# Mixing of the first block redrawn: heads in pairs, a new column order, and a new order of work on three engines

## The reference, cut to what matters

```python
for l in range(2):                                   # first block
    proj = rms_norm(x, ln1) @ w_in                   # 1024 -> 23 column chunks of 128
    mq, mk = rope(rms_norm(mq)), rope(rms_norm(mk))  # per head of 64
    y_moba = causal softmax attention, 6 heads       # one block of 256 keys
    qk = silu(causal_conv4(xqk));  i, f gates
    num = (q k^T * w) v;  den = sum(q k^T * w)       # w = exp(d - m_t), mLSTM, 4 heads
    h = num / max(|den|, exp(-m_t))
    y_mlstm = rms_norm(h * sigmoid(xo)) per head
    y_swa = windowed softmax attention with sinks, 6 query heads, 2 key heads
    x = x + concat(y_moba, y_mlstm, y_swa) @ w_out   # 8 row slabs of w_out
    x = x + relu(rms_norm(x) @ w_up)^2 @ w_down
```

## Time and profile before

| | us |
|---|---|
| three timed runs | 1591.03, 1581.5, 1591.17 (median 1591.03) |
| the profiled execution, its own time | 1587.58 |
| its span, from the first to the last instruction | 1585.7 |

### The profile page before, as it was taken

The page is one execution under the profiler, slowest core; times in us unless marked ns, Lnnn a source line. Parts: engine busy times, 40 slices in busy tenths (PEclk is TensorE's granted clock), DMA queues, the critical chain, the costliest instruction groups (busy, mean ns, idle before and its releaser), DMA issues.

```text
span 1585.7 us, 25621 instructions
## 1 busy us (share of the span) xinstructions
PE 1492.0 (94%) x10380; PEld 1366.3 (86%) x10380; DVE 1175.4 (74%) x1911; ACT 830.5 (52%) x1256; POOL 10.5 (1%) x21
## 2 busy tenths in 40 slices
PE   6987899999887999999999999999999999999997
PEld 5875788888875678888999899999899999999996
DVE  6677788886767778887756787788776678777753
ACT  4453577634444567644536555444554666455542
POOL 2000000000000000000000000000000000000000
PEclk9997999999898999999999999999999999999999
DMA  8441279996432159997745557789975555578662
GB/s 216 124 134 49 83 221 265 271 295 181 120 107 80 54 175 259 261 306 233 227 134 155 151 160 213 222 242 256 261 218 171 147 147 161 171 228 228 193 181 76
DMA packets 480422, 292.29 MB, mean 184 GB/s; under 512 B 13725, under 2 KB 452257, under 8 KB 480049
## 3 DMA queue, kind: packets, MB, share of 16 engines
q1 hardware_dynamic: 478928, 287.02, 63.0%
q10 hardware_dynamic: 672, 1.97, 0.3%
q0 software_dynamic: 704, 1.66, 0.3%
HBM read 289.56 MB, written 1.05 MB: 183 GB/s over the span
## 4 chain that ended last, share of the span: by engine, by line
PE 68%; DVE 20%; ACT 7%; issue 4%; DMA 0%; ACTq 0%; DVEq 0%
PE acc L1453 10%; PE mx L1470 10%; PE acc L1454 10%; PE acc L1455 10%; PE acc L1470 7%; DVE w_lo L815 6%; PE mx L1471 5%; PE acc L1471 4%; ACT w_hi L498 3%; DVE ada_acc L902 2%; PE mx L1501 1%; PE mx L1722 1%; PE mx L1711 1%; ACT gt L785 1%; DVE upv L1396 1%
## 5 line engine op out<-in xcount | busy, mean ns | idle before, releaser
L815 DVE TENSOR_TENSOR w_lo<-raw,w_hi 128x1024 fp32r<-128x1024 f32 x450 | 547.4, 1220 | 168.3 <-ACT w_hi L498 167.0
L1453 PE MATMUL acc<-h,w_hi 128*128 128x258 f32 (+1 forms) x1776 | 521.6, 294 | 11.8 <-DVE w_lo L815 9.7
L1454 PE MATMUL acc<-h,w_hi 128*128 128x258 f32 (+1 forms) x1776 | 508.4, 286 | 0.0
L1455 PE MATMUL acc<-h,w_lo 128*128 128x258 f32 (+1 forms) x1776 | 502.8, 283 | 0.0
L498 ACT ACTIVATE w_hi<-raw 128x1024 fp32r<-128x1024 f32 x450 | 460.3, 1047 | 37.2 <-DMA raw<-in_w_down 15.9
L1453 PEld LDWEIGHTS acc<-h,w_hi 128*128 128x128 f32 x1776 | 340.4, 192 | 23.6 <-DVE w_lo L815 10.1
L1454 PEld LDWEIGHTS acc<-h,w_hi 128*128 128x128 f32 x1776 | 341.2, 192 | 6.7 <-issue 6.3
L1455 PEld LDWEIGHTS acc<-h,w_lo 128*128 128x128 f32 x1776 | 343.4, 193 | 0.0
L1470 PE MATMUL mx<-u,w_hi 128*128 128x512 f32 x864 | 302.3, 394 | 2.1 <-DVE u L1402 2.1
L1471 PE MATMUL mx<-u,w_lo 128*128 128x256 f32 x864 | 241.5, 280 | 0.0
L1470 PEld LDWEIGHTS mx<-u,w_hi 128*128 128x128 f32 x864 | 162.2, 188 | 37.5 <-DVE u L1402 2.5
(11 more groups left out here) (272 smaller groups left out, 1731.8 us busy)
## 6 DMA issues: line engine op xcount, KB each, us to landing
raw<-in_w_in SPq DMA_DIRECT2D x132, 512.0 KB, 3.9
ada<-in_w_ada SPq DMA_DIRECT2D x96, 512.0 KB, 5.0
raw<-in_w_ffn_in SPq DMA_DIRECT2D x88, 512.0 KB, 4.6
raw<-in_w_up SPq DMA_DIRECT2D x64, 512.0 KB, 4.6
raw<-in_w_down SPq DMA_DIRECT2D x64, 512.0 KB, 5.3
raw<-in_w_out SPq DMA_DIRECT2D x32, 512.0 KB, 3.8
raw<-in_w_ffn_out SPq DMA_DIRECT2D x32, 512.0 KB, 4.5
raw<-in_w_ret_o SPq DMA_DIRECT2D x16, 512.0 KB, 4.0
```

The lines of the kernel that those rows point to most:

```text
L815: V.tensor_tensor(w_lo[:, n % NS], raw[:, n % NS], w_hi[:, n % NS].bitcast(F32), ALU.subtract).then_inc(lo_ready, 1)
L1453: mm(outp, w_hi[:, i % NS, k], rhs[:, k, 0], start=k == 0, stop=False)
L1454: mm(outp, w_hi[:, i % NS, k], rhs[:, k, 1], start=False, stop=False)
L1455: ins = mm(outp, w_lo[:, i % NS, k], rhs[:, k, 0], start=False, stop=k == KT - 1)
```

## The change

It is made in the mixing of the first block, in both layers.

- **Columns.** `A_ORDER` brings the chunks of the attention pairs earlier and mixed with the values. In `proj` the two chunks of a head-norm group now lie side by side (`A_PLACE`), and the swa keys are paired with another chunk. Projections use three `acc` banks; the fourth, `acc[:, 3]`, takes the sums, the partners and two of the values, one after the other.
- **Pairs.** Attention goes by six pairs of heads in the order 0, 1, 2, 4, 3, 5. Both heads of a pair have their matmuls interleaved (rows 0 to 63 and 64 to 127 of the array, or columns 0 to 63 and 64 to 127), one exponential phase, one set of maxima, six transposes into two banks, one copy. ml_scores and ml_outputs go by two heads as well.
- **Masks on PSUM.** A matmul of the rounded identity with the masks opens each bank of scores, and the scores are added to it. Maxima are read from PSUM (one reduction over 2 x 3 x 128), and the exponential reads PSUM too. The masks are loaded and rounded once, on ACT in layer 0.
- **Memory without division.** The root-mean-square norm of num / max(|den|, e) is taken without the quotient: m_d = max(den^2, e^2), v = sum(h^2) + 64 eps m_d, h * v^-1/2. The reciprocal and two passes go; `g_E` is exp(-2 G), clamped on DVE (`f_E2`). The first tap of the convolution moves to ACT (`conv_first`), the rounding of y_hi 3 and 4 as well.
- **Order.** The head norms, the memory and pairs 0 and 1 stand between the projections; pair 2 between `out_chunks`, of which slabs 0 to 3 first go with six of eight chunks. Slabs 6 and 7 go bank by bank at the end.
- **Constants.** The decay table shares its place with the masks' neighbours in `con` and is loaded in the MLP of layer 1, by the queue of GpSimd.

```diff
-A_ORDER = (22, 14, 15, 16, 17, 20, 21, 18, 19, *range(14))
+A_ORDER = (22, 14, 15, 16, 17, 20, 21, 0, 3, 18, 19, 1, 4, 6, 7, 2, 5, 8, 13, 10, 12, 9, 11)
+PAIRS = (0, 1, 2, 4, 3, 5)
+W_ORDER = (3, 4, 0, 1, 2, 6, 5, 7)
```

On ACT:

```diff
+                def conv_first(k):
+                    act.wait_ge(ap_ev, e0 + 2 + k)
+                    nc.scalar.activation(cv[:, k], proj[:, A_PLACE[C_XQK + k]], ACT.Identity, scale=vec(V_CONVW + l * 16 + 12 + k),
+                                         bias=vec(V_CONVB + l * 4 + k)).then_inc(cv_first, 1)
...
+                ahead(21)
+                head_square(2)
+                exps(0)
+                head_seed(2)
+                ahead(22)
+                turned(0)
```

On DVE:

```diff
+                def maxima(j):
...
+                    c.link(V.tensor_reduce(st_mx[:, i], mx[:, 0:2, 0:384].rearrange("p n (b k) -> p n b k", b=3), AX, ALU.max))
+                    c.link(V.tensor_tensor(st_mx[:, i, :, 1:2], st_mx[:, i, :, 1:2], st_mx[:, i, :, 2:3], ALU.max))
...
-                c.link(V.scalar_tensor_tensor(r_tmp[:], mx[:, 3], -1.0, ebc, ALU.mult, ALU.max))
-                c.link(V.tensor_tensor(r_tmp[:], mx[:, 3], r_tmp[:], ALU.max))
...
-                c.link(V.reciprocal(r_tmp[:], r_tmp[:]))
...
+                c.link(V.tensor_tensor(m_d, m_d, ebc[:], ALU.max))
+                to_sbuf(14)
+                head_norm(1)
+                dve.wait_ge(ml_ss, l + 1)
+                V.scalar_tensor_tensor(m_v, m_d, HD * EPS, mx[:, 0], ALU.mult, ALU.add).then_inc(ml_v, 1)
...
+                to_sbuf(16)
+                maxima(0)
+                rope(1)
...
+                to_sbuf(17)
+                probabilities(0)
+                head_norm(2)
+                to_sbuf(18)
+                maxima(1)
+                to_sbuf(19)
+                outputs(0)
+                rope(2)
+                probabilities(1)
...
+                maxima(3)
                 rope(4)
...
+                lo_upto(p0 + 29)
+                probabilities(3)
+                maxima(4)
+                lo_upto(p0 + 30)
+                outputs(3)
+                probabilities(4)
+                maxima(5)
+                outputs(4)
+                lo_upto(m0 + 1)
+                probabilities(5)
+                outputs(5)
```

On PE:

```diff
+                    for i in range(2):
+                        mm(mx[:, i, 0:384], ident_r[:], masks[:, 0:384] if p < 3 else masks[:, 384:768], start=True, stop=False)
+                    for a, t, n in ((0, 0, P), (P, P, S)):
+                        for i in range(2):
...
+                project(9)
+                sums(0)
+                project(10, 11)
...
+                project(17)
+                sums(2)
+                turn(0)
                 project(18)
+                at_outputs(0)
+                at_scores(1)
                 project(19)
+                partners(2)
+                turn(1)
                 project(20)
...
+                turn(3)
+                pe.wait_ge(qk_sin, l * 5 + 5)
+                for w in range(4):
+                    out_chunks(w, 6, 8).then_inc(slab_used, 1)
+                at_outputs(3)
+                at_scores(4)
+                out_chunks(4, 0, 8).then_inc(slab_used, 1)
+                turn(4)
+                at_outputs(4)
+                at_scores(5)
+                out_chunks(5, 0, 8).then_inc(slab_used, 1)
+                turn(5)
+                at_outputs(5)
```

More of the change, by code:

```diff
@@ L624, in _ @@
-                ahead(14)
-                weights(2)
-                ahead(15)
-                weights(3)
+                weights(1)
+                ahead(13)
+                head_square(0)
+                ahead(14)
+                head_seed(0)
+                ahead(15)
+                weights(2)
+                weights(3)
+                values(0)
+                ahead(17)
+                head_square(1)
+                act.wait_ge(ml_nd, l * 4 + 4)
+                nc.scalar.activation(m_d, mx[:, 3], ACT.Square).then_inc(ml_d, 1)
@@ new lines, in turn @@
+                def turn(j):
+                    pe.wait_ge(at_p, l * 6 + j + 1)
+                    if j:
+                        pe.wait_ge(at_y, l * 6 + j)
+                    else:
+                        pe.wait_ge(ml_h, l + 1)
+                        pe.wait_ge(ml_d, l + 1)
+                    for i in range(2):
+                        for a in (0, P, 2 * P):
+                            ins = nc.tensor.transpose(mx[:, 2 + i, a:a + P], pr[j % 2][:, i, a:a + P], ident)
+                    ins.then_inc(at_t, 1)
@@ new lines, in at_outputs, with v @@
+                def at_outputs(j):
+                    p = PAIRS[j]
+                    pe.wait_ge(at_pt, l * 6 + j + 1)
+                    if j == 0:
+                        pe.wait_ge(v_sb, l * 3 + 2)
+                    if j == 2:
+                        pe.wait_ge(v_sb, l * 3 + 3)
+                    def v(i, t):
+                        if p < 3:
+                            return vtok[:, 1 + p // 2, 2 * (p % 2) + t, i * HD:(i + 1) * HD]
+                        kv = (2 * (p - 3) + i) // 3
+                        return vtok[:, 2, 2 + t, kv * HD:(kv + 1) * HD]
+                    for bank, t, a, first, last in ((2, 0, 0, True, True), (3, 0, P, True, False), (3, 1, 2 * P, False, True)):
+                        for i in range(2):
+                            ins = mm(mx[i * HD:(i + 1) * HD, bank, 384:512], v(i, t), pT[:, i, a:a + P], start=first, stop=last)
+                    ins.then_inc(at_o, 1)
@@ new lines, in _ @@
+                at_outputs(3)
[7 more added lines that the diff above has]
+                at_outputs(5)
+                pe.wait_ge(lo_ready, o0 + 8)
+                for b in range(4):
+                    ins = out_chunks(6, 2 * b, 2 * b + 2)
+                    if b == 3:
+                        ins.then_inc(slab_used, 1)
+                    out_chunks(7, 2 * b, 2 * b + 2).then_inc(slab_used if b == 3 else bank_done, 1)
```

624 lines of the change are left out of this document (307 added, 317 removed).

## The result

The changed kernel takes 1629.76 us (median of four executions, 1629.6 to 1638.49); the kernel before, 1590.18 beside it. The ratio is 1.0275, 95% interval 1.0225 to 1.0324. The forecast was 1620, the range 1580 to 1648, and slower had 0.65.

The account below looks back on a forecast made before the run. TensorE was taken as the bound, busy 94% of the span. To 1587.6 us came 8.2 for layer 0, 6.1 for layer 1 and 16.2 for the clock, 1618.1, stated as 1620 after the runs' median; range 1580 to 1648.

Parts of the forecast that it names:

- PE's own work: Layer 0 mixing from the first memory broadcast: PE's matmuls without waits sum to 113.7 us, against 138 busy before.
- DVE and ACT keep up: Faster rival, chance 0.13: mixing waits stay at 27 us, 17.8 less per layer, 1552 us in all.
- points 1 to 8: PE's waits on DVE and ACT along layer 0's mixing, from g_E's clamp to turn(5) and its outputs; 53 us.
- the walk: Following PE, DVE and ACT queues through layer 0's new order at full clock: 166.9 us against 157.8, layer +8.2.
- six of the ten at 1.35, 8.1 a layer: Of ten mixing waits over 3 us per layer, six cost 1.35 us each by slower matmuls; bounds 0 and twice that.
- The end and layer 1: Free MLP slab 6.1 us after the last w_out matmul, not 6.8; layer 1 +6.1 us, layer 0 +8.2.
- the clock term: Loss from PE's lower granted clock after long mixing waits, both layers: 16.2 us in all.
- Six groups of transposes at 3 to 6 us: Sign: PE idles 3 to 6 us before each probability transpose group, six per layer, released by DVE.
- The wait before the first sum by ACT: Sign: PE waits about 5 us before the first sum of squares in the mixing, released by ACT.
- Cold: Rival, chance 0.08: clock stays low from turn(0) on, +18 us per layer, 1656 us.
- Pairs don't overlap: Rival, chance 0.07: paired heads' matmuls do not run in parallel, 14 us more PE work, +8 a layer, 1636 us.
- Even: Rival, chance 0.20: ordering waits overcharged or clock stays full; 1602 us without the clock term, about 1590 with waits at 45.

Follow-up runs that it names:

- E1: Changed kernel with PE order alone altered: slab 18 before turn(0) and slab 20 before turn(1); 1616.55 us, ratio 1.0172.
- E3: Changed kernel with DVE and ACT order of pairs 3 to 5 alone altered (w_hi, w_lo, swap copy and output_hi earlier); 1609.90 us, ratio 1.0123.
- E4: Changed kernel with the orders of E1, E2 and E3 and further moves at the other waits, same instructions; 1568.23 us, ratio 0.9860.
- E8: E4 with four more moves of order, before sums(2), turn(1) and turn(3); 1554.52 us, ratio 0.9781.
- E5: Changed kernel, order kept, with useless matmuls on PE in its nine long waits per layer; 1610.55 us, ratio 1.0134.
- E9: E8 with maxima(0) before rope(1) on DVE and exps(0) before the rounding of the memory's y on ACT; 1558.20 us, ratio 0.9787.
- E10: E9 with slab 6 of w_out done whole before slab 7, which alone goes bank by bank; 1556.00 us, ratio 0.9782.
- E7: E4 with head 1's matmuls after head 0's instead of alternating, in scores and outputs of attention and memory; 1573.19 us, ratio 0.9896.
- E2: Changed kernel with DVE order alone altered: probabilities(0) before the eviction of chunk 17 and its w_lo; median 1631.35 us, ratio 1.0230.
- E11: Kernel before the change with 88 useless matmuls per layer on PE at five places; 1585.84 us, ratio 0.9968.

## Why the prediction was right, point by point

**Direction and cause.** Right: DVE and ACT in program order make PE wait, and the waits moved on to slabs at the lower clock. E1, E3, E4 and E8 show it, since order alone takes 75 us from the kernel. In sum, layer 0 lost 24.0 us (178.9 and the 2.9 of the slab that moved out of the piece, against 157.8): 22.5 more of waiting and 13.8 more of slow work, less 12.3 of PE's own work (129.1 to 116.8, worked out below). The rival "DVE and ACT keep up" fell as written, though its own mark, waits under about 44 us per layer, was missed by little (45.6 and 44.5): the waits alone nearly cancel what PE saves, and the rest of the loss comes with the lower clock. Its arithmetic (1552 with the waits at 27) is near what E8 reached, 1554.5 with waits of 20 us per layer; what it took was another order.

**The waits, points 1 to 8.** Walked 53.2 us for layer 0, measured 45.6. The large ones fit: turn(0) 6.4 against 6.11, turn(1) 5.3 against 5.17, at_scores(0) 3.4 against 3.40, turn(2) 3.5 against 3.14, turn(3) 4.9 against 4.78, partners(4) 3.2 against 2.89. Too high were sums(0) (5.3, measured 3.72), sums(2) (3.8, 1.12: PE came to it late from slabs at the lower clock, and the wait of the walk was spent as slow work; in E5, at a higher clock, it is 3.65), and turn(4) and turn(5) with outputs (5.9 and 6.9, 5.57 each). In E5 idle time (18.8) and filler (254 matmuls at 0.12) together are some 49 us, so by this estimate the walk was 4 too high at nearly full clock.

**PE's own work.** 113.7 us; E8, which has much less of the lower clock, has 139.0 - 19.6 waits - 5.5 lost by slabs, and the slab that moved out of the piece is 2.9: 116.8. So 3.1 too low per layer, at most: E8's small matmuls behind its two longest waits were slow as well, by some 2.3 us, which this sum counts as work. The prices that were short, from the timeline of E8 (outputs 0.81 and scores 0.86 as taken, masks 0.63 where I took 0.36):

```profile
139.54 0.88 PE L1716 MATMUL mx<-pT,vtok 128*64 128x128 f32 x12
140.35 0.39 PE L1542 MATMUL acc<-y,w_hi 128*128 128x256 f32 x1
...
142.84 0.70 PE L1676 MATMUL mx<-masks,ident_r 128*128 128x384 f32 x2
143.47 0.93 PE L1685 MATMUL mx<-proj 64*128 64x128 f32 x8
144.33 0.39 PE L1542 MATMUL acc<-y,w_hi 128*128 128x256 f32 x1
```

Elsewhere the masks take 0.54 and the six transposes 0.57 to 0.71, so a pair is 2.8 to 2.9 and not 2.6: 1 to 2 per layer. A 512-column float32 matmul is 0.94 to 0.95 where a small matmul follows (0.85 taken, read where a slab follows), at most 1.1 for eleven. The statement that by PE's work alone the change would win 20 us was wrong by its base: I set 113.7 against 138 us of busy time, in which matmuls overlap and slow ones count long. Like for like, the piece before less waits and low slabs is 157.8 - 23.1 - 5.6 = 129.1, and the new work 116.8: 12 us per layer.

**The clock, the term that was mis-sized in the layer.** The step was "six of the ten at 1.35, 8.1 a layer". With the work of E8 (113.9, without the moved slab), the changed layer 0 has 178.9 - 45.6 - 113.9 = 19.4 us of slow work, more than twice the 8.1 and above the upper bound of 16.2. In layer 0 each wait of over 2 us but the one before partners(4) was followed by slow matmuls, the small ones among them: six transposes took 1.2 from start to start instead of 0.6 to 0.7, the two broadcasts of g_E 1.84 instead of 1.06. By its effect on the time the term held better: E5 took 19.2 us away in all, where 16.2 were forecast. That slow work in part ran in the place of a wait would explain both this and the waits being shorter than walked; no run separates the two.

The price itself was read from one case. The earlier trace rows has a slow slab behind a wait of 2.86 us in layer 1; in layer 0 the same step waits as long, and the granted clock is 1.00 from 87.78 to the end of the slab behind it at 91.50:

```profile
87.78 1.13 PE L1654 MATMUL mx<-sqq,con 128*128 128x512 f32 x2 [2.85 <-ACT sqq L630]
```

**The end and layer 1.** The free MLP slab came 5.0 us (225.34) after the last w_out matmul (forecast 6.1), but the bank-wise slab 6 has little part in it: that distance is 6.0 us in E9 and 6.5 in E10. Layer 1 lost 20 us against 23 in layer 0, near the 2.1 less of the forecast. (The walk's sum for layer 0 is 166.9 - 157.8 - 0.7 = 8.4, not 8.2; this changes nothing.)

**The sum.** 1620 against 1629.8. Of the 9.8, the clock term is 3.0, by E5; the walk, +14.3 at full clock, should have been near 1610.6 - 1589.4 = 21, and the 7 between is in part PE's work, at most 3.1 per layer; no run shows it alone. That the total came so near is partly luck. In layer 0 the forecast is 166.9 + 8.1 = 175.0 and the measured time 181.8, with the slab that moved: the waits 7.6 too high, the slow work 11.3 too low and PE's work 3.1 too low, so two errors of opposite sign cancel in part; without the one in the waits the sum would have been some 15 us further off.

**The signs named ahead.** Six groups of transposes at 3 to 6 us: yes (3.1 to 6.1). The wait before the first sum by ACT: 3.7 us in layer 0, and the 5.0 forecast in layer 1. Clock lower: yes. The last w_out matmul 175 us after the broadcast: 178.9, and 181.8 with the slab that the forecast counted in. PE busy near 120 us: no, 140, since busy time grows with the lower clock; that was a bad sign to name.

**The other rivals.** "Cold": the clock did not stay at 0.5, but the slow work of layer 0, 19.4 us, is nearer to this rival's 25 than to my 8.1; by its effect on the time, 9.6 per layer in E5, it is nearer to mine. "Pairs don't overlap": refuted by the prices under E7 (0.85 us for one head's scores and for two). "Even": refuted.

**Still open.** What each part costs by itself (masks on PSUM, memory without division, first tap on ACT) was not tried; E4 and E8 only show that together they are no loss. Nor is it known why one execution of E2 got the better clock.

## What to carry to other kernels

A change of operations that comes with a new order is to be judged in two parts: walk each in-order queue to every wait of the engine that is the bound, and ask for each what it stands behind; here the slower kernel and the faster one have the same instructions, and about twenty statements moved turned a ratio of 1.0275 into 0.9781. Before a wait on the bounding engine, put work that is ready (a slab), and on its suppliers put what the wait needs before what fills buffers ahead. Count the lower clock behind the waits too, and after removing one look at the granted clock before believing the gain.

## What the runs showed of the hardware

- Work that computes nothing of use, put into waits, made the kernel faster by 19 us of 1630 (E5), and by 5 of 1591 in the kernel before (E11).
- One kernel can have different mean clocks from execution to execution: E2 had 0.947 to 0.949 in three, of 1631 to 1632 us, and 0.959 in one, of 1617.
- Two sets of matmuls with 64 rows on different halves of the array overlapped fully, though issued one whole set behind the other (0.86 us in E7, 0.85 alternating in E4, 0.85 for one set alone in the kernel before); with 64 columns on different halves they overlapped in part (1.07 against 0.81 alternating; one head alone took 0.80 in the kernel before, 156.95 to 157.75). The Trainium skill (TensorEngine Tiling (Array Packing), Tiling Modes) says that tiles operate independently and makes no difference between the two; the rows agree for the first and in part for the second.
- Two float32 matmuls of only 4 rows by 256 columns (four records in the trace) took 1.84 us behind a wait of 2.01 us, from 49.06 on, at a granted clock of 0.57, and 1.06 in E8, behind a wait of 0.44, at 1.00.
